# A two-block transformer kernel: the partition sums of the modulation vector as two rounded products, with the operations around them in other places

## The reference, cut to what matters

```python
c_act = jax.nn.silu(c)                          # (1, 2048)
mod = jnp.dot(c_act, w_ada[l]) + b_ada[l]       # w_ada: (2048, 12288)
sh1, sc1, g1, sh2, sc2, g2 = jnp.split(mod, 6, axis=-1)
```

## The kernel before, in words

| groups | tiles added during | sum on TensorE |
|---|---|---|
| 0 | output projection | gate and up, round 0, ahead of chunk 1 |
| 1 to 10 | gate and up, rounds 0 to 9 | the next round, ahead of chunk 1 |
| 11 | gate and up, round 10 | in the middle of chunk 2 of down |
| 12 to 18 | down | in the middle of a chunk of down; 18 between its last half chunks |
| 19 | pgate | after chunk 12 |
| 20 to 23 | expert blocks 48 to 111 | after the next block; 23 one block later |

## Time and profile before

### The profile page before, as it was taken

One profiled execution on the slowest core, in us unless ns is written; L12 is line 12 of the kernel. 1 busy time (PEld: TensorE's weight loads), 2 busy tenths in 40 slices (PEclk: granted clock), 3 DMA queues, 4 the chain that ended last, 5 costly groups with the idle time before them and its releaser, 6 DMA issues.

```text
span 3195.8 us, 43133 instructions
## 1 busy us (share of the span) xinstructions
PE 3118.2 (98%) x16202; PEld 2635.4 (82%) x16202; DVE 2253.3 (71%) x2657; ACT 1415.6 (44%) x1416; POOL 718.5 (22%) x513
## 2 busy tenths in 40 slices
PE   8999899999999998999979999999999999999997
PEld 6888788888877776888769888888888888888886
DVE  7766788888888888456688888766665555555556
ACT  5556543333334455446554444443334344344342
POOL 1100000000000000000001888888882101100100
PEclk9999999999999998999989999999999999999999
DMA  8444577777789874684335777888876766676762
GB/s 280 180 173 184 219 273 275 276 281 276 277 300 334 299 256 177 220 328 152 141 124 172 236 214 219 257 257 259 257 236 219 253 243 248 245 255 237 256 242 112
DMA packets 195358, 754.24 MB, mean 236 GB/s; under 512 B 53826, under 2 KB 53858, under 8 KB 124850
## 3 DMA queue, kind: packets, MB, share of 16 engines
q1 hardware_dynamic: 129988, 664.86, 57.6%
q0 software_dynamic: 55904, 70.92, 8.1%
q10 hardware_dynamic: 9360, 17.04, 1.4%
HBM read 714.82 MB, written 37.93 MB: 236 GB/s over the span
## 4 chain that ended last, share of the span: by engine, by line
PE 90%; DVE 5%; ACT 2%; issue 2%; DMA 2%; DVEq 0%; SPq 0%; ACTq 0%
PE bank L430 27%; PE bank L424 15%; PE bank L426 15%; PE bank L425 15%; PE bank L431 14%; PE bank L928 1%; ACT ffn_hi L1451 1%; DMA ring<-in_first 1%; PE bank L827 1%; DVE misc L2190 0%; PE bank L536 0%; DVE raw_lo L2028 0%; PE bank L864 0%; DMA ring<-in_down 0%; DVE raw_lo L2315 0%
## 5 line engine op out<-in xcount | busy, mean ns | idle before, releaser
L430 PE MATMUL bank<-h_both,ffn_hi 128*128 128x512 f32 x3440 | 1198.3, 395 | 0.0
L2723 DVE TENSOR_TENSOR part_lo<-ring,ffn_hi 128x2048 fp32r<-128x2048 f32 x256 | 586.9, 2293 | 328.7 <-ACT ffn_hi L1915 322.4
L430 PEld LDWEIGHTS bank<-h_both,ffn_hi 128*128 128x128 f32 x3440 | 645.6, 188 | 160.9 <-issue 12.1
L1915 ACT ACTIVATE ffn_hi<-ring 128x2048 fp32r<-128x2048 f32 x252 | 482.8, 1916 | 625.4 <-PE bank L431 389.8
L3041 POOL DMA_INDIRECT weight_dram<-misc x256 | 561.6, 2194 | 87.9 <-issue 75.4
L431 PE MATMUL bank<-h_both,part_lo 128*128 128x256 f32 x2048 | 567.3, 277 | 0.0
L424 PE MATMUL bank<-ffn_hi,coef_hi 128*128 128x512 f32 x1024 | 398.4, 389 | 1.0 <-DVE coef_lo L2874 1.0
L426 PE MATMUL bank<-ffn_hi,coef_lo 128*128 128x512 f32 x1024 | 398.4, 389 | 0.0
L425 PE MATMUL bank<-part_lo,coef_hi 128*128 128x512 f32 x1024 | 398.3, 389 | 0.0
L431 PE MATMUL bank<-h_both,raw_lo 128*128 128x256 f32 x1392 | 386.5, 278 | 0.0
L431 PEld LDWEIGHTS bank<-h_both,part_lo 128*128 128x128 f32 x2048 | 384.5, 188 | 0.0
(11 more groups left out here) (439 smaller groups left out, 5010.3 us busy)
## 6 DMA issues: line engine op xcount, KB each, us to landing
ring<-in_u_table SPq DMA_DIRECT2D x128, 1024.0 KB
ring<-in_v_table SPq DMA_DIRECT2D x128, 1024.0 KB
misc<-in_w_ada SPq DMA_DIRECT2D x192, 512.0 KB
ring<-in_gateup SPq DMA_DIRECT2D x88, 1024.0 KB
ring<-in_first SPq DMA_DIRECT2D x56, 1024.0 KB
ring<-in_down SPq DMA_DIRECT2D x44, 1024.0 KB
ring<-in_stream SPq DMA_DIRECT2D x40, 1024.0 KB
ring<-in_wo_pq SPq DMA_DIRECT2D x32, 1024.0 KB
```

The lines of the kernel that those rows point to most:

```text
L430: nc.tensor.matmul(out[:, 0:2 * S], hi, x_pair, start=start, stop=False)
L1915: a.activation(part_hi[j % PARTS], raw[j % RAW], ACT.Copy).then_inc(sem("hi_ready"), 1)
L2723: v.tensor_tensor(part_lo[j % PARTS], raw[j % RAW], part_hi[j % PARTS].bitcast(F32), ALU.subtract).then_inc(sem("lo_ready"), 1)
```

## The change

The 24 sums are computed in another form. `ones` is a rounded tile now (`ones_r`, 128x128). ScalarE rounds the complete tile `ada_acc` into `ada_hi` (`ada_upper`, 128x512), VectorE writes the rest into `ada_lo` (the new `ada_end`, in place of the memset), and TensorE sums both by `ones_r` with two rounded products of 128x512. The sum now lands on all 128 partitions of the bank, of which `ada_row` reads the first as before. The next group's k = 0 waits for `ada_end` instead of for the sum. In down, sum and end stand one chunk later, behind the chunk's low part, and `ada_row` too; in pgate the sum stands after the first half of chunk 13; in the expert stage `ada_end` stands one block later. Place and number of all other operations are unchanged.

```diff
+        ones_r = rounded("ones_r", "ones", 0, P)[:, :]
+        ones = ones_r.bitcast(F32)
...
-            def ada_sum(g, acc=ada_acc):
+            def ada_sum(g, hi=ada_hi, lo=ada_lo):
 
                 pe.wait_ge(sem("ada_sum"), g + 1)
-                m = pe.matmul(ada_bank(g)[0:1, 0:ADA_W], ones[:, 0:1], acc, start=True, stop=True)
-                m.then_inc(sem("ada_rowsum"), 1)
+                pe.matmul(ada_bank(g)[:, 0:ADA_W], ones_r, hi, start=True, stop=False)
+                pe.matmul(ada_bank(g)[:, 0:ADA_W], ones_r, lo, start=False, stop=True).then_inc(sem("ada_rowsum"), 1)
...
-                    if m == down_ada_ends(g) - 1:
+                    if m == down_ada_ends(g):
...
-            ada_sum(ADA_FFN)
             for j in range(13, 16):
                 m = pgate_chunk(j, (0,))
+                if j == 13:
+                    ada_sum(ADA_FFN)
...
+            def ada_upper(g, acc=ada_acc, hi=ada_hi):
+
+                a.wait_ge(sem("ada_used"), ADA_SLOTS + KD * g + KD)
+                a.wait_ge(sem("ada_rowsum"), g + 1)
+                a.activation(hi, acc, ACT.Copy).then_inc(sem("ada_rounded"), 1)
...
                 upper_in(N_IN + 3 + i)
+                if i == 11:
+                    ada_upper(0)
...
                         else:
                             down_upper(c - uppers)
+                ada_upper(ADA_EARLY + it)
...
                 if k == 0:
-                    v.wait_ge(sem("ada_rowsum"), g + 1)
+                    if not isinstance(g, int) or g:
+                        v.wait_ge(sem("ada_sum"), g)
...
-            def ada_end(g):
-                v.wait_ge(sem("ada_used"), ADA_SLOTS + KD * g + KD)
-                v.memset(mxs[:, 0, 1:2], 0.0).then_inc(sem("ada_sum"), 1)
+            def ada_end(g, acc=ada_acc, hi=ada_hi, lo=ada_lo):
+
+                v.wait_ge(sem("ada_rounded"), g + 1)
+                v.wait_ge(sem("ada_rowsum"), g + 1)
+                v.tensor_tensor(lo, acc, hi.bitcast(F32), ALU.subtract).then_inc(sem("ada_sum"), 1)
...
             some_ada(12)
+            lower_in(N_IN + 12)
             ada_end(0)
-            lower_in(N_IN + 12)
...
-                    if m == down_ada_ends(g) + 2:
+                    if m == down_ada_ends(g) + 3:
                         ada_row(g)
...
                 down_lower(m)
+                for g in ended:
+                    ada_end(g)
...
+                i = j - ADA_U_FIRST
                 lower(j + PARTS - 1)
+                if i in range(KD, ADA_U_STEPS + 1, KD):
+                    ada_end(ADA_U + i // KD - 1, ada_acc_u, ada_hi_u, ada_lo_u)
                 dots_summed(j)
```

More of the change, by code:

```diff
@@ L153, in build_program @@
         ident = sb("ident", [P, P])
-        ones = sb("ones", [P, P])
+        sb("ones", [P, P])
+        ones_r = rounded("ones_r", "ones", 0, P)[:, :]
+        ones = ones_r.bitcast(F32)
         rope_t = sb("rope_t", [P, T, 2 * (ROT_A + ROT_B)])
@@ L199, in build_program @@
         mod_row = misc[:, 5120:5120 + ADA_W]
+        ada_hi, ada_lo = (rounded(n, "misc", at, ADA_W)[:, :] for n, at in (("ada_hi", 4608), ("ada_lo", 5632)))
+        ada_hi_u, ada_lo_u = (rounded(n, "aux", at, ADA_W)[:, :] for n, at in (("ada_hi_u", 2560), ("ada_lo_u", 3072)))
         ada_ring_u = misc[:, 2048:2048 + ADA_SLOTS * ADA_W].rearrange("p (s c) -> p s c", s=ADA_SLOTS)
@@ L308, in build_program @@
                   "rec_scan", "rec_sum", "rec_sq", "row_in", "ssq_in", "resid_piece", "silu_done",
-                  "ada_used", "ada_sum", "ada_rowsum", "mod_ready", "mod_b_in", "mod_out",
+                  "ada_used", "ada_rounded", "ada_sum", "ada_rowsum", "mod_ready", "mod_b_in", "mod_out",
                   "cact_ready", "modc_in", "misc_in", "lat_ready", "rope_done", "rotq_ready",
@@ L1373, in _ @@
                 dots_of_block(first + KD, 0) if g == ADA_G - 1 else None
-                ada_sum(g, ada_acc_u)
+                ada_sum(g, ada_hi_u, ada_lo_u)
             for j in range(ADA_U_FIRST + ADA_U_STEPS + 2, NEB):
@@ L1674, in _ @@
                 down_upper(m)
+                for g in range(ADA_DOWN, ADA_FFN):
+                    if m == down_ada_ends(g):
+                        ada_upper(g)
             def pgate_upper(j):
@@ L1738, in _ @@
                     pgate_upper(j)
+                if j == 13:
+                    ada_upper(ADA_FFN)
             def n5_half(t, first, last):
@@ L1937, in _ @@
                     choice_exp(EXP_AT[j])
-            done = WOVEN // PARTS - 1
-            with loop(a, NEB // PARTS - 2 - done) as it:
+            for g in range(ADA_U, ADA_G):
+                with loop(a, KD // PARTS) as it:
+                    for j in range(PARTS):
+                        upper(WOVEN + (g - ADA_U) * KD + PARTS + j, it)
+                        gelu(WOVEN + (g - ADA_U) * KD + j, it)
+                ada_upper(g, ada_acc_u, ada_hi_u)
+            with loop(a, (NEB - WOVEN - ADA_U_STEPS) // PARTS - 1) as it:
                 for j in range(PARTS):
-                    upper((2 + done) * PARTS + j, it)
-                    gelu((1 + done) * PARTS + j, it)
+                    upper(WOVEN + ADA_U_STEPS + PARTS + j, it)
+                    gelu(WOVEN + ADA_U_STEPS + j, it)
             def coefficients_hi(q, it=0, first=False):
@@ L1987, in roots @@
                 link(v.reciprocal(st[:, dst:dst + n], got))
-            v.memset(ones[:, :], 1.0).then_inc(sem("ones_set"), 1)
+            v.memset(ones, 1.0).then_inc(sem("ones_set"), 1)
             mark(v.memset(xrT[:, :, 0:2], 0.0))
@@ L2340, in _ @@
                 for g in range(ADA_DOWN, ADA_FFN):
-                    if m == down_ada_ends(g) + 2:
+                    if m == down_ada_ends(g) + 3:
                         ada_row(g)
+                ended = [g for g in range(ADA_DOWN, ADA_FFN) if m == down_ada_ends(g)]
                 for i in down_ada(m):
-                    ada(i % KD, ADA_DOWN + i // KD)
-                    if i % KD == KD - 1:
-                        ada_end(ADA_DOWN + i // KD)
+                    if not ended or ADA_DOWN + i // KD == ended[0]:
+                        ada(i % KD, ADA_DOWN + i // KD)
                 down_lower(m)
+                for g in ended:
+                    ada_end(g)
+                    for i in down_ada(m):
+                        if ADA_DOWN + i // KD > g:
+                            ada(i % KD, ADA_DOWN + i // KD)
             for g in range(ADA_DOWN, ADA_FFN - 1):
-                if down_ada_ends(g) + 2 >= DOWN:
+                if down_ada_ends(g) + 3 >= DOWN:
                     ada_row(g)
@@ L2438, in _ @@
                     ada(2 * (j - 5) + 1, ADA_FFN)
-                if j == 12:
+                if j == 13:
                     ada_end(ADA_FFN)
@@ L2883, in _ @@
                     coefficients(0)
-                i = j - ADA_U_FIRST
                 if i == 0:
@@ L2894, in _ @@
                     ada(i % KD, ADA_U + i // KD, ada_ring_u, ada_acc_u)
-                    if i % KD == KD - 1:
-                        ada_end(ADA_U + i // KD)
             lower(NEB + PARTS - 1)
```

## The result

| | before | changed |
|---|---|---|
| runs (us) | 3196.76, 3204.07, 3203.69, 3197.50 | 3238.69, 3233.87, 3238.88, 3233.75 |
| median of these | 3200.6 | 3236.28 |
| profiled execution, span | 3195.8 | 3236.9 (its time: 3238.69) |
| granted TensorE clock, mean | 0.987 | 0.983 |

The changed kernel takes 1.0107 times as long, 95% interval 1.009 to 1.0124. The forecast was 3226 with a range of 3210 to 3243.

A forecast was written before the change was run, and what follows sets the result against it. TensorE, 98% busy and nearly gapless, was taken as the bound. 24 + 4.3 - 9.7 - 0.8 = +17.8 us, with the clock +26.1, gave 3222.9 to 3229.8 us: forecast 3226, range 3210 to 3243.

The forecast's parts named there:

- Gate and up, ten waits of 2.4 us (+24): In gate and up, ten sums wait for a tile rounded behind a load-bound weight rounding, 2.4 us later each: +24 us.
- rival 3: Loads at a round's end and of chunk 14 land early enough: -12.4 us, 3188 us; chance 0.06.
- rival 4: Pauses give DMA time, loads land 1.8 us sooner, a round costs 0.6 us: 3200 us; chance 0.10.
- The clock (+8.3): Five of ten gate and up waits each lower TensorE's clock to 0.50 for 3.3 us, costing half: +8.3 us.
- Rival 1: The waits come but the clock hardly falls: +17.8 us, say 3218 us; chance 0.22.
- rival 2: The clock falls in nearly every wait or stays down longer: +34 us, 3234 us; chance 0.12.
- The pair, 0.69 us less: On TensorE, two rounded products take 0.46 us in place of 1.15; 14 of 24 sums save 9.7 us.
- the 14 sums at 0.69: Sums with both parts ready in time, groups 0 and 11 to 23, saving 0.69 us each: 9.7 us.
- Output projection (+4.3): At the output projection's end, the tile's late rounding delays VectorE's low parts and the phase ends later: +4.3 us, once.
- the second wait near 364: In the output projection, a TensorE wait of 2 us near 364, for chunk 15's low part.
- Down (-0.8): In down, VectorE no longer waits for the sum, so a low part TensorE waited for comes earlier: 0.8 us saved.

The follow-up runs named there:

- e1: Changed kernel with ScalarE rounding the tile ahead of the last weight rounding in each round of gate and up; 3200.77 us, ratio 0.9997.
- e3: Changed kernel with TensorE's sum in gate and up one chunk later, ahead of chunk 2 and not chunk 1; 3195.94 us, ratio 0.9974.
- a2: The changed kernel itself, run again for a second profile; 3233.34 us, ratio 1.0091.
- e5: e1 plus first tile rounded one chunk earlier in the output projection, and VectorE's tile low part before each gate-and-up round's last chunk's; 3189.01 us, ratio 0.9957.
- e4: e1 plus first tile rounded one chunk earlier in the output projection, but the sum as one fp32 product that VectorE's k = 0 waits for; 3225.73 us, ratio 1.0067.
- e0: The kernel before, unedited, run again for a second profile; 3205.74 us, span 3204.2 us.
- e7: e5 with one column of the rounded ones as the weights of both products of a sum; 3196.45 us, ratio 0.9981.
- e6: e3 with the first tile's rounding one chunk earlier in the output projection; 3193.81 us, ratio 0.9967.
- e8: e5 with one small fp32 product, 128x1 by one column, ahead of the pair in each sum; 3203.05 us, ratio 1.0001.

## Why the prediction was right, point by point

- **Gate and up, ten waits of 2.4 us (+24): right.** The round of 545.42 has the predicted chain (load, weight rounding, tile's rounding, low part, pair), and the experiments undo it at two different links: e1 by ScalarE's order, e3 by TensorE's. From the product ahead of a sum to the second behind it the ten took 39.6 us together, before 15.0: +24.6. Two of the five clock falls began before the pair and add about 1.1 us to these 24.6, so the waits alone are 23.5. The load follows the end of a chunk and came no sooner, which kept rival 3 and rival 4 out. The trace agrees with the Trainium skill (TensorE: Matmul & The Clock Gate, section on the array's architectural detail) that ScalarE takes its operations in order: the tile was complete at 539.87 and was rounded at 544.03, only behind the weight rounding that waited for its load, and in e1, written ahead of it, it was done (538.05) 1.55 us before that load had landed (539.60).
- **The clock (+8.3): right.** Five of ten, 3.41 us each, half of it lost: 8.5 us. Without the waits (e1, e3) none fell in gate and up. Rival 1 and rival 2 are out, and a2 has five again, which cost 10.2 us. Which five is not explained: the waits with and without a fall have the same length. The prediction took five as the middle of none and ten, so that the number fits so well is partly luck.
- **The pair, 0.69 us less: right where it stands in the stream.** 0.46 in down and in e5; in the retrieval 0.80 to 0.83 from the product ahead to the second behind, before 1.50. Group 0 was counted among the 14 sums at 0.69 and gained 0.27 (1.22 us, before 1.49).
- **Output projection (+4.3): the sum right (+4.2), its parts not.** One wait of 2.15 us came and a clock fall of 3.41 us (1.7), for which this term had nothing; the second wait near 364 didn't come. That the sum fits is luck. (Ahead of the projection the changed kernel was 0.8 us early, hence the 3.4 at the start of gate and up.)
- **Down (-0.8): not as predicted.** VectorE's waits for the sum ahead of k = 0 went and so did the wait at 1111.79. But another of 2.15 us came at 1162.90, and TensorE waits 3.7 us in all (before 3.8):

```profile
PE bank L428 <- DVE raw_lo L2342: 3.7, 2, 2.2
```

 What was gained at one low part was given back at another. That one (1160.57 to 1162.85) stood in VectorE's list behind other work without a pause; VectorE's last pause ahead of it, 0.69 us at 1149.54, was for a rounding that had waited for its load. The stage as a whole fits by chance: predicted 5.5 + 0.8 = 6.3 us, measured 7.1 (a2 6.7). Eight sums are 5.5 of it, and 1.6 stay open. That the edit there was needed at all is shown by e4: without the new wait of k = 0, the later place costs 15 us of waits.
- **Missing: the pace, at nothing in the sum.** The two profiles differ by 41.1 us and not 26.1. Of the 15 us between, the retrieval has 10.5 (+7.7 where its four sums should have saved 2.8; the pace makes 10.2 there), gate and up 2.4 (34.0 against 31.6; the pace makes 3.3), and the stages between down and the retrieval 3.7. In those the clock stood at 0.50 for 20.48 us from 1342.2 on, before for 13.65 from 1314.9 on, and TensorE fell back by 3.2 us in that stretch; in a2 it was 13.65 again and the stages took 505.0, so this isn't the change's. The rest is -1.6: 0.8 less in down and 0.8 ahead of the projection. Of the pace's 10.2 in the retrieval, 6.9 came in e0 too, so at most the rest is the change's.

The forecast was 10 us low, inside its range. By the medians the change cost 35.7 us in the first comparison and 27.9 in that of a2 (ratios 1.0107 and 1.0091, intervals that overlap), where the prediction added up 26.1. So part of the 10 us belongs to which executions were measured; what the pace makes of the medians isn't shown, as there are two profiles of each kernel.

## What to carry to other kernels

An operation that is put at the end of an in-order engine's list is not done when its input is ready but when the load of the operation ahead of it has landed; look for the engine's idle time ahead of that place, not for its busy share. A consumer one chunk later, or a producer ahead of the waiting load, is worth more than the cheaper instruction: here +34.0 us became -3.4 (e3) or +2.1 (e1) in gate and up. When a consumer is moved later, see who waits for it in turn (e4). And before a few us of a TensorE-bound kernel are put down to an edit, count the products in equal windows of both profiles.

## What the runs showed of the hardware that was not expected

- The same stream of products, at granted clock 1.00 and without idle time, runs at 0.347 or 0.353 us a pair (1.9%), and keeps to one for up to 450 us. Behind the fp32 column sum of 128x512 it was 0.347 in ten of the eleven rounds of gate and up in three profiles (before, e0, e4), and 0.353 in the first, which the expectation of e7 overlooked; in the retrieval it was 0.347 behind each such sum. Behind a rounded pair with 128 columns it changed at some sums and not at others, in e3, e5 and e6 in a regular turn: two rounds at 0.347, two at 0.353. With a pair of one column, or a small fp32 product ahead of the pair, it was 0.353 in all rounds of gate and up, and changed in the retrieval. What selects it stays open: neither the data format of the sum nor its columns of weights accounts for all of these.
- The stretch of the retrieval ahead of its first sum was at either pace in the same kernel (before 0.347, e0 0.353), worth 6.9 us; this explains most of the 8.4 us between their profiles.
- Waits of TensorE of 2.6 to 2.9 us in a dense stream of products, followed by 3.41 us at granted clock 0.50 in half of the cases: five of ten in each of the two profiles of the changed kernel, one of the falls twice as long.
- An fp32 product of a single column between rounded ones costs 0.33 us (e8), three quarters of a whole rounded pair of 128x512.
